# Gate and up products of two of four row blocks by Strassen's seven products, in every repeated FFN block

## The reference

```python
def swiglu(h, w_gate, w_up, w_down):
    return (jax.nn.silu(h @ w_gate) * (h @ w_up)) @ w_down
...
        h = rms_norm(x, norm_ffn_pre[layer])
        f = swiglu(h, ffn_w_gate[layer], ffn_w_up[layer], ffn_w_down[layer])
        x = x + rms_norm(f.astype(x.dtype), norm_ffn_post[layer])
```

## Time and profile before

| | |
|---|---|
| time, median of three | 2271.08 us |
| time of the profiled execution | 2270.22 us |
| span of its records | 2268.4 us |
| busy PE / weight load / DVE / ACT / POOL | 99 / 82 / 58 / 46 / 8 % of the span |
| granted TensorE clock, mean | 0.999 |
| matmul records | 10251 |
| HBM traffic | 412.73 MB read, 183 GB/s over the span |

### The profile page before, as it was taken

The page is one execution under the profiler, slowest core; times in us unless marked ns, Lnnn a source line. Parts: engine busy times, 40 slices in busy tenths (PEclk is TensorE's granted clock), DMA queues, the critical chain, the costliest instruction groups (busy, mean ns, idle before and its releaser), DMA issues.

```text
span 2268.4 us, 27348 instructions
## 1 busy us (share of the span) xinstructions
PE 2249.3 (99%) x10251; PEld 1855.5 (82%) x10251; DVE 1311.4 (58%) x1412; ACT 1048.6 (46%) x1222; POOL 174.3 (8%) x197
## 2 busy tenths in 40 slices
PE   9999999999999999999999999999999999999998
PEld 7888888888888888888787888778888888888886
DVE  5576567555555555555746555776545555554555
ACT  6677545533333343333655555446334333333432
POOL 0941001000000000000121001010000000000001
PEclk9999999999999999999999999999999999999999
DMA  9455444655655655555464444556555555555553
GB/s 317 167 177 167 167 144 143 233 186 189 198 187 185 195 193 185 188 198 187 149 204 150 156 159 149 186 167 204 186 194 194 187 189 195 189 185 192 193 188 111
DMA packets 213832, 415.81 MB, mean 183 GB/s; under 512 B 12328, under 2 KB 14976, under 8 KB 213248
## 3 DMA queue, kind: packets, MB, share of 16 engines
q1 hardware_dynamic: 213040, 414.29, 55.4%
q10 hardware_dynamic: 720, 0.56, 0.1%
HBM read 412.73 MB, written 2.10 MB: 183 GB/s over the span
## 4 chain that ended last, share of the span: by engine, by line
PE 96%; DVE 1%; DMA 1%; SPq 1%; issue 0%; ACT 0%; POOLq 0%; POOL 0%; DVEq 0%; ACTq 0%
PE acc L1046 90%; PE tp L1060 2%; PE sc L1140 1%; DMA raw<-in_ev_w_in 1%; PE pv L1169 1%; PE sc L1136 1%; PE pv L1164 1%; DVE w_lo L1234 1%; PE sc L1119 0%; PE pv L1119 0%; DVE xs L1272 0%; SPq L654 0%; SPq L643 0%; DVE h_lo L1247 0%; DVE yacc L1289 0%
## 5 line engine op out<-in xcount | busy, mean ns | idle before, releaser
L1234 DVE TENSOR_TENSOR w_lo<-raw,w_hi 128x2048 fp32r<-128x2048 f32 x381 | 875.3, 2300 | 491.9 <-PE acc L1046 462.8
L775 ACT ACTIVATE w_hi<-raw 128x2048 fp32r<-128x2048 f32 x381 | 730.6, 1918 | 764.2 <-PE acc L1046 730.7
L1046 PE MATMUL acc<-w_hi,h_hi 128*128 128x512 f32 x2216 | 604.2, 394 | 4.2 <-ACT h_hi L821 2.7
L1046 PE MATMUL acc<-w_hi,h_lo 128*128 128x512 f32 x2216 | 593.5, 390 | 1.5 <-DVE h_lo L1247 1.4
L1046 PE MATMUL acc<-w_lo,h_hi 128*128 128x512 f32 x2216 | 593.1, 389 | 0.6 <-DVE w_lo L1234 0.6
L1046 PEld LDWEIGHTS acc<-w_hi,h_lo 128*128 128x128 f32 x2216 | 415.4, 188 | 89.7 <-DVE h_lo L1247 2.7
L1046 PEld LDWEIGHTS acc<-w_lo,h_hi 128*128 128x128 f32 x2216 | 415.9, 188 | 88.7 <-DVE w_lo L1234 1.0
L1046 PEld LDWEIGHTS acc<-w_hi,h_hi 128*128 128x128 f32 x2216 | 409.5, 188 | 87.4 <-issue 7.1
L1289 DVE TENSOR_TENSOR yacc<-acc,yacc 128x512 f32<-128x512 f32 x208 | 141.7, 687 | 170.5 <-PE acc L1046 170.5
L1046 PE MATMUL acc<-w_hi,y_hi 128*128 128x512 f32 x832 | 224.5, 392 | 0.7 <-ACT y_hi L977 0.7
L1046 PE MATMUL acc<-w_lo,y_hi 128*128 128x512 f32 x832 | 222.6, 389 | 0.0
(11 more groups left out here) (172 smaller groups left out, 1075.8 us busy)
## 6 DMA issues: line engine op xcount, KB each, us to landing
raw<-in_ffn_w_gate SPq DMA_DIRECT2D x88, 1024.0 KB, 5.1
raw<-in_ffn_w_up SPq DMA_DIRECT2D x88, 1024.0 KB, 5.1
raw<-in_ffn_w_down SPq DMA_DIRECT2D x88, 1024.0 KB, 5.0
raw<-in_od_w_in SPq DMA_DIRECT2D x48, 1024.0 KB, 5.1
raw<-in_ev_w_in SPq DMA_DIRECT2D x37, 1024.0 KB, 5.5
raw<-in_ev_w_out SPq DMA_DIRECT2D x16, 1024.0 KB, 5.0
raw<-in_od_w_out SPq DMA_DIRECT2D x16, 1024.0 KB, 5.0
raw<-in_ev_w_in SPq DMA_DIRECT2D x12, 256.0 KB, 6.5
```

The source lines that it names most:

```text
L775: act.activation(w_hi[u % HI][:, :, :], raw[u % RAW][:, :, :], ACT.Copy).then_inc(hi_done, 1)
L1046: mm = pe.matmul(acc[n % 2][t][:, :], operand(lhs, a, k, t), w[:, k, :], start=first and k == 0 and j == 0, stop=last and k == KT - 1 and ...
L1234: dve.tensor_tensor(w_lo[u % LO][:, :, :], raw[u % RAW][:, :, :], w_hi[u % HI][:, :, :].bitcast(F32), ALU.subtract).then_inc(lo_done, 1)
```

## The change

Take rows of h in two halves of 128 tokens, columns of h (rows of the weights) in four groups kg = 0 to 3. For kg 0 and 1 the four blocks of h and the four blocks g0, g1 (gate), u0, u1 (up) form a 2 x 2 by 2 x 2 product. Before, that is four units, eight halves. After, seven products P1 to P7 (the Strassen-Winograd form) take their place, each a half of 12 matmuls (`single`). g2, g3, u2, u3 and the four down units stay as they were.

- Weights: P5, P6, P7 and P4 use u0 - g0, u1 - (that), u1 - u0 and g1 - (P6's weight). DVE makes each from `raw` in place (`form`, 128x2048), then ACT and DVE split it as any unit. So a block has 15 entries to split (P1 to P7 and eight units), not 12, and four forms.
- Left operands: four sums of h's blocks, S1 to S4, are made once a layer by POOL (`left_sums`, eight additions of 128x512) and split by ACT and DVE (`left_high`, `left_low`).
- Results: P1 and P5 go to the banks `sc` and `pv` and are copied out by ACT; P6 and P7 are added to P1 by DVE (`second`, `third`); POOL adds P5 to both sums (`spreads`, two 128x512); P3, P2 and P4 accumulate in `acc` with the dense units; DVE adds the sums at the four `corner`s; silu and gating follow from SBUF.
- Loads: the same twelve per block in the order LOADS, over five buffers in turn, the two new ones on memory that attention used (`gx` and `queries`). A buffer is free when its last reader is done.
- The loops are written out. In a layer's first block the transposes come after P5.
- The tasks of the head change: `head_end` adds the form of P5 and the four splits of S1 to S4.

```diff
+BLOCK_RAW = 5
...
+ENTRIES = ("P1", "P5", "P3", "P6", "g2", "P2", "P7", "P4", "u3", "g3", "u2", "d0", "d1", "d2", "d3")
+LOADS = ("u1", "u0", "g0", "g2", "g1", "u3", "g3", "u2", "d0", "d1", "d3", "d2")
+FORMS = ("P5", "P6", "P7", "P4")
+SUMS = ("S2", "S3")
+PLAIN = {"P1": "g0", "P2": "g1", "P3": "u1"}
...
+def head_end(slots, body):
+    def left(name):
+        return Task("sums", 2 * body.layer + 1, body.layer, what=name)
+    tasks = []
+    for i, s in enumerate(slots):
+        last = len(slots) - 1 - i
+        tasks += half(s, 0)
+        tasks += [hi(u) for u in range(ahead(s.u - 1, HI_LEAD), min(ahead(s.u, HI_LEAD), body.base + 1))]
+        tasks += [lo(u) for u in range(ahead(s.u - 1, LO_LEAD), min(ahead(s.u, LO_LEAD), body.base + 1))]
+        if last == 1:
+            tasks += [Task("form", src=body, what="P5"), hi(body.base + 1), lo(body.base + 1)]
+        if last == 0:
+            tasks += [left("S1"), left("S3")]
+        tasks += half(s, 1) + s.post
+    return tasks + [left("S2"), left("S4")]
...
+    def take(key, buffers, released):
+        nonlocal order
+        buf = min(buffers, key=lambda i: age[i])
+        count[buf] += 1
+        plan.place[key] = Place(buf, count[buf], free[buf])
+        free[buf] = released
+        order += 1
+        age[buf] = BLOCK_RAW + order
...
+            released = {"g0": (lo_of["P4"],), "u0": (lo_of["P7"],), "u1": (lo_of["P3"], form_of["P7"]),
+                        "g1": (lo_of["P2"], form_of["P4"])}
+            for name in LOADS:
+                take((body.index, name), range(BLOCK_RAW), released.get(name) or (lo_of[name],))
...
+            def load(key, src):
+                place = plan.place[key]
+                for what, value in place.free:
+                    sp.wait_ge(lo_done if what == "lo" else form_done, value)
...
+                sp.wait_ge(s_done, plan.heads_of[part.layer])
...
+            def hi(u, formed=0):
+                place = plan.place[u]
+                if formed:
+                    act.wait_ge(form_done, formed)
+                else:
+                    act.wait_ge(landed[place.buf], 16 * place.count)
                 if u >= HI:
-                    act.wait_ge(unit_done, u - HI + 1 + 12 * it)
...
+                def copy_first():
+                    act.wait_ge(unit_done, body.u["P1"] + 1)
+                    if body.first:
+                        act.wait_ge(left_lo_done, len(LEFT) * (body.layer + 1))
+                    act.activation(spare[0], product1, ACT.Copy).then_inc(copied[0], 1)
...
+                def copy_fifth():
+                    act.wait_ge(unit_done, body.u["P5"] + 1)
+                    if body.first:
+                        act.wait_ge(left_lo_done, len(LEFT) * (body.layer + 1))
+                    else:
+                        act.wait_ge(tok_ready[1], body.index)
+                    act.activation(spare[3], product5, ACT.Copy).then_inc(copied[1], 1)
...
+                def silu_low():
+                    wait_acc(act, body.gate, 0)
+                    stage_wait(body, 0)
+                    act.activation(stage[:, 0, :], spare[0], ACT.Silu, scale=rstd_x[:, 0:1]).then_inc(silu_done[0], 1)
...
+                high("P3")
+                high("P6")
+                high("g2")
+                copy_first()
+                block_hi(body)
+                high("P2")
+                high("P7")
+                high("P4")
+                high("u3")
+                high("g3")
+                high("u2")
+                high("d0")
+                silu_low()
+                copy_fifth()
+                high("d1")
+                high("d2")
+                high("d3")
+                silu_high()
+                high_next("P1")
+                high_next("P5")
+                if not body.next:
+                    hi(body.base + len(ENTRIES) + 2)
...
+            def single(u, bank, a_hi, a_lo, start, stop):
+                hi_tile, lo_tile = w_hi[u % HI], w_lo[u % LO]
+                pe.wait_ge(hi_done, u + 1)
+                for j, (a, w) in enumerate(((a_hi, hi_tile), (a_hi, lo_tile), (a_lo, hi_tile))):
+                    if j == 1:
+                        pe.wait_ge(lo_done, u + 1)
+                    for k in range(KT):
...
+                def open_bank(body, name, column, t):
+                    if name == first_of(column, t):
+                        n = body.gate if column == "g" else body.up
+                        pe.wait_ge(acc_free[n % 2][t], n // 2)
+                        if t:
+                            pe.wait_ge(sum_done, body.sum["S2" if column == "g" else "S3"])
+                        return True
+                    return False
...
+                    if not body.first:
+                        turn()
+                    for name in ENTRIES:
+                        if name == "P1":
+                            if not body.first:
+                                pe.wait_ge(copied[0], body.index)
+                            formed(body, name, product1, rows(0, 0), True, True)
+                        elif name == "P5":
+                            if not body.first:
+                                pe.wait_ge(copied[1], body.index)
+                            formed(body, name, product5, None, True, True)
+                            if body.first:
+                                turn()
+                        elif name == "P6":
+                            pe.wait_ge(acc_free[1][1], body.gate // 2)
+                            formed(body, name, acc[1][1][:, :], None, True, True)
+                        elif name == "P7":
+                            pe.wait_ge(acc_free[0][1], body.up // 2)
+                            formed(body, name, acc[0][1][:, :], None, True, True)
+                        elif name == "P2":
+                            formed(body, name, acc[1][0][:, :], rows(1, 0), open_bank(body, name, "g", 0), name == last_of("g", 0))
+                        elif name == "P4":
+                            formed(body, name, acc[1][1][:, :], rows(1, 1), open_bank(body, name, "g", 1), name == last_of("g", 1))
+                        elif name == "P3":
+                            formed(body, name, acc[0][0][:, :], None, open_bank(body, name, "u", 0), name == last_of("u", 0))
+                        elif name[0] == "d":
+                            down(body, int(name[1]))
+                        else:
+                            dense(body, name)
...
+                if name == "P5":
+                    up = weight("u0")
+                    dve.tensor_tensor(g0, up, g0, ALU.subtract).then_inc(form_done, 1)
+                elif name == "P6":
+                    dve.tensor_tensor(g0, weight("u1"), g0, ALU.subtract).then_inc(form_done, 1)
+                elif name == "P7":
+                    up = weight("u0")
+                    dve.tensor_tensor(up, weight("u1"), up, ALU.subtract).then_inc(form_done, 1)
+                else:
+                    dve.tensor_tensor(g0, weight("g1"), g0, ALU.subtract).then_inc(form_done, 1)
...
+                def second():
+                    dve.wait_ge(unit_done, body.u["P6"] + 1)
+                    dve.wait_ge(copied[0], body.index + 1)
+                    if not body.first:
+                        dve.wait_ge(spread, 2 * body.index)
+                    dve.tensor_tensor(spare[1], acc[1][1][:, :], spare[0], ALU.add).then_inc(sum_done, 1)
+                def third():
+                    dve.wait_ge(unit_done, body.u["P7"] + 1)
+                    dve.wait_ge(sum_done, body.sum["S2"])
+                    dve.tensor_tensor(spare[2], acc[0][1][:, :], spare[1], ALU.add).then_inc(sum_done, 1)
+                def corner(column, t, other, out):
+                    n = body.gate if column == "g" else body.up
+                    wait_last(dve, body, column, t)
+                    if (column, t) != ("g", 0):
+                        dve.wait_ge(spread, 2 * body.index + (1 if (column, t) == ("u", 0) else 2))
+                    dve.tensor_tensor(out, acc[n % 2][t][:, :], other, ALU.add).then_inc(acc_free[n % 2][t], 1)
+                def gated(t):
+                    wait_acc(dve, body.up, t)
+                    dve.wait_ge(silu_done[t], body.index + 1)
+                    dve.wait_ge(tp_done, body.e + t + 1)
+                    dve.scalar_tensor_tensor(tok[:, t, :], spare[3 if t else 1], rstd_x[:, t:t + 1], stage[:, t, :],
+                                             ALU.mult, ALU.mult).then_inc(tok_ready[t], 1)
...
+                form(body, "P6")
+                low("P3")
+                low("P6")
+                low("g2")
+                form(body, "P7")
+                second()
+                low("P2")
+                form(body, "P4")
+                low("P7")
+                low("P4")
+                low("u3")
+                third()
+                low("g3")
+                low("u2")
+                corner("g", 0, spare[0], spare[0])
```

(82 more changed lines are left out.)

296 lines of the change are left out of this document (196 added, 100 removed).

## The result

The changed kernel takes 2231.81 us, the median of four runs (2231.47 to 2234.35), against 2271.24 of the kernel before: a ratio of 0.9829, with a 95% interval of 0.9812 to 0.9846. The forecast was 2227, with a range of 2213 to 2244: right in sign and range, 4.8 us too low. The profiled execution is the longest of the four, 2234.35 us, 2232.6 of it the span.

What follows compares the result with a forecast made beforehand. PE, busy 99% of the span, was taken as the bound: 2270.2 - 54.4 (matmuls) - 1.4 (transposes) + 11.2 (first-block waits) = 2225.6; the median lies 0.9 above, 2226.5, so 2227 us, eight in ten from 2213 to 2244.

Steps and rivals of the forecast that it cites:

- The saving on PE, 54.4 us: In 10 blocks of 2 layers, seven products for eight remove 2.72 us of PE matmuls a block, 54.4 us in all.
- 12 matmuls x 0.2267: The product saved in each block, 12 matmuls at the old pace of 0.2267 us each, is 2.72 us of PE time.
- Straight code and the transposes in the first block: Unrolled code costs PE nothing; transposes no longer right behind the gating give 1.4 us back over both layers' first blocks.
- DVE's 52.7 us a block: DVE's work per block: 19 large operations, 16 small ones and 2 gatings, 52.7 us of a 63.45 us block, 83%.
- The walk of the block: One steady block timed: no PE waits, least slacks 1.4 us at P7's split and 0.9 us at u's corner.
- the rival of a wait in every block: Waits of 0.5 to 1.5 us in each of 18 later blocks, 9 to 27 us more, 2236 to 2254; chance 0.19.
- DVE as the bound: Rival: slower large DVE operations make blocks exceed 66.17 us; at 2.8 us each, 2309 us, slower than before; chance 0.05.
- The first blocks, 11.2 us given back: In each layer's first block g0 queues behind u1 and u0, so PE waits: 6.1 and 5.1 us, 11.2 in both.
- the 0.3 at P7: In a layer's first block PE waits 0.3 us more at P7, by the same walk, part of the 6.1 us.
- The rival of no return here: The first blocks give no time back, since queue order is read from one place per layer: 2215 us; chance 0.18.
- The clock: Rival: PE's waits in the first blocks drop its clock to half, an estimated 4 us a layer, 2235 us; chance 0.08.
- a granted clock under 0.99: The sign named in advance that the clock rival, PE's clock falling in the first blocks, holds.

Runs made afterwards that it cites:

- the runs with more work: Changed kernel plus needless DVE reductions ahead of P7's split in every block: about 1.2 us of them, 2233.49 us; about 2.2 us, 2249.79 us.

## Why the prediction was right, and where it was off

- **The saving on PE, 54.4 us**: right. At the full pace the block is 63.45 us to the hundredth, in every kernel whose `lefts` starts on a multiple of 256 bytes. In the changed kernel it is 63.65. The step that failed is "12 matmuls x 0.2267", which took the pace of the old operands for the new one as well: 24 matmuls a block cost 8 ns more each, 4 us of the 4.8 that the forecast was low. None of my rows had a stationary operand off that alignment, and I put no bound on it.
- **Straight code and the transposes in the first block**: right. Unrolling is worth 1.0002.
- **DVE's 52.7 us a block**: 53.57. POOL added nothing to it. The forecast took every operation by its step from start to start; DVE pauses nine times in a block, and the operation ahead of a pause counts in full, some 0.09 us more (2.29 for 2.20). A form costs a split, 2.28 to 2.29 us.
- **The walk of the block**: right at both of its narrow places. P7's slack is 1.4 us in the trace, and the runs with more work bound it from 1.2 to 1.5. At the corner of u it is 1.1 (ends 601.3, bank wanted at 602.4) for a forecast of 0.9. So the rival of a wait in every block, given 0.19, fell, as did DVE as the bound.
- **The first blocks, 11.2 us given back**: the mechanism, SP's queue, is shown by the reordered loads. The size by starts is 10.3 us: 5.9 in layer 0 (69.57 less 63.65; forecast 6.1) and 4.4 in layer 1 (69.39 less 63.65, less 1.3 of the clock; forecast 5.1). By starts, PE waited 1.3 us for S1's rest there where I had put 1.6, and 2.8 for P3's where I had put 3.2; the 0.3 at P7 hardly came in either layer. The rival of no return here, given 0.18, fell.
- **The clock**, a rival given 0.08: it came beside the forecast, not instead of it, in one of the two first blocks of the profiled run, 1.3 us for an estimate of 4 a layer, and once more at the start, where I had not looked for it, 1.6 us. The sign that I had named for it, a granted clock under 0.99, is too coarse: the mean of after is 0.997. The estimate took all matmuls between the waits at half pace and did not see that a fall ahead of a wait costs nothing.
- **The start, +4.4 us in the profiled run**: not forecast; 1.6 us of it are the clock, the rest is not explained. PE's first transposes of layer 0's mixer come at 50.59 us in before and 54.98 in after, but at 51.50 to 54.75 in the other changed kernels, and at 52.12 in before unrolled, so much of it differs between executions of nearly the same code up to there. The latest two, 54.98 and 54.75, are those whose clock fell just ahead of the transposes. The profiled span is 8.8 us over the forecast's: 4.4 of the start, 4.0 of the tile, 1.3 of the clock in layer 1, less 0.9 for the shorter waits. By medians, 2231.8 against the sum's 2226.5, it is 5.3, of which the last three give 4.4.

## What to carry to other kernels

Where PE bounds a kernel and its engines feed it through queues, a hand walk of one steady block in steps from start to start finds slacks to a few tenths of a microsecond; the same walk at the block that follows other code finds where a load's place in the queue, not its size, is paid for. Look at the order of loads wherever a change makes the first entry of a block need something else first: here the order was worth 7.5 us by the medians, a fifth of what the change gave. Place every tile that serves as stationary operand on a multiple of 256 bytes (0 and 256 past a multiple of 512 were tried, and are fast), and judge an alignment theory only after trying coarse steps.

## What the runs showed of the hardware that I had not expected

- With a stationary operand of 128x128 fp32r that starts 96 bytes past a multiple of 512, matmuls of 512 columns start every 0.233 to 0.234 us; at 128 past it every 0.230 to 0.233; at 0 and 256 past it every 0.2267.
- The granted clock fell to 1.2 GHz behind waits of PE of under 3 us in the middle of a busy run, in 15 of 18 first blocks with two waits of 1.1 to 2.7 us, in one with a single wait of 2.2 us, and in none of five with a single wait of 1.2 to 1.3 us. At the start of after it fell behind waits of 0.7 and 1.1 us.
- An addition of 128x512 on POOL of 1.29 us takes 2.0 to 3.3 beside large two-input work of DVE in SBUF, and in the steady block ends 1.2 us after the split beside it.
